# Small constants in one table, squares further ahead, warming matmuls, sums and gate product on POOL, last unit in quarters

## What is computed

```python
h = rmsnorm(x, g_mix)
u, q, k, v, og, zr, ga, gb = split(h @ w_in, (512, 256, 256, 512, 512, 16, 1024, 1024))
# branch A: four channel groups of u, trailing means over 2, 4, 8, 16 tokens minus the token,
pool = (((csum[t] - csum[t-w]) / w - u) @ w_group) * scale ; y_a = pool @ w_pool_proj
# branch B: gated linear attention, 4 heads, chunks of 64
loga = log_sigmoid(zr @ w_gk_up + b_gk) / 16 ; o = gla(q, k, v, loga, state)
y_b = (headnorm(o) * g_gla_norm * silu(og)) @ w_gla_proj
x = x + (sigmoid(ga) * y_a + sigmoid(gb) * y_b) @ w_out
x = x + (silu(gate) * up) @ w_ffn_out          # gate, up = rmsnorm(x, g_ffn) @ w_ffn_in
y = rmsnorm(x, g_final)                        # and the new pooling rows and GLA states
```

## Time and profile before

| | us |
|---|---|
| three runs: median (lowest, highest) | 910.1 (909.24, 910.98) |
| profiled execution, its own time | 910.94 |
| its span on the slowest core, 7 | 909.7 |
| spans of the other cores | 903.1 to 909.2 |
| PE busy / DVE / ACT / POOL on core 7 | 875.3 / 438.2 / 259.8 / 106.9 |

### The profile page before, as it was taken

How to read it: one execution, slowest core, us unless ns; L and a number is a source line. 1 busy time by engine, 2 the same in 40 slices (tenths; PEclk the granted TensorE clock), 3 DMA queues, 4 the chain that set the end, 5 groups by cost and what they waited for, 6 DMA issues and landing times.

```text
span 909.7 us, 14454 instructions; the slowest of 8 cores (903.1 to 909.7 us)
## 1 busy us (share of the span) xinstructions
PE 875.3 (96%) x4868; PEld 446.4 (49%) x4868; DVE 438.2 (48%) x735; ACT 259.8 (29%) x512; POOL 106.9 (12%) x214
## 2 busy tenths in 40 slices
PE   2898999999999999999999999999999999999996
PEld 1444556664565566556644444444444444444442
DVE  4578665656634422432256665565561332232146
ACT  4454343222332122112226524332231011101122
POOL 4300111102100000100022001120120000000002
PEclk9999999999999999999999999999999999999998
DMA  8964453828736916660875995343774753262504
GB/s 161 239 124 93 75 104 70 145 53 156 117 74 114 191 54 116 116 139 24 144 127 193 196 216 94 65 69 48 127 113 80 128 93 63 55 115 47 93 24 162
DMA packets 57627, 100.49 MB, mean 110 GB/s; under 512 B 41858, under 2 KB 42626, under 8 KB 50260
## 3 DMA queue, kind: packets, MB, share of 16 engines
q0 software_dynamic: 10272, 66.61, 41.3%
q1 hardware_dynamic: 47284, 32.96, 14.6%
HBM read 139.36 MB, written 11.53 MB: 166 GB/s over the span
## 4 chain that ended last, share of the span: by engine, by line
PE 92%; DMA 2%; DVE 2%; issue 2%; ACT 1%; POOL 1%; DVEq 0%; ACTq 0%; POOLq 0%
PE ps L419 88%; DMA ring<-w_a 2%; DVE R L316 1%; DVE R L320 1%; PE ps L763 1%; PE ps L744 0%; PE ps L541 0%; PE ps L721 0%; ACT R L310 0%; PE ps L764 0%; PE ps L532 0%; ACT R L312 0%; PE ps L1043 0%; ACT sgt L310 0%; PE ps L655 0%
## 5 line engine op out<-in xcount | busy, mean ns | idle before, releaser
L419 PE MATMUL ps<-hT,ring 128*128 128x368 bf16 (+2 forms) x2720 | 508.2, 344 | 5.8 <-ACT sgt L310 2.3
L419 PEld LDWEIGHTS ps<-hT,ring 128*128 128x128 bf16 x2720 | 261.2, 98 | 234.3 <-issue 12.6
L310 ACT ACTIVATE sgt<-ps 128x368 f32<-128x368 f32 (+2 forms) x207 | 109.6, 531 | 434.8 <-PE ps L419 374.1
L419 PE MATMUL ps<-ring,R 128*128 128x512 bf16 (+1 forms) x1020 | 222.5, 379 | 0.0
L316 DVE TENSOR_TENSOR R<-ps,sgt 128x368 bf16<-128x368 f32 (+1 forms) x110 | 66.1, 602 | 236.3 <-PE ps L419 228.9
L419 PEld LDWEIGHTS ps<-ring,R 128*128 128x128 bf16 (+1 forms) x1020 | 100.5, 99 | 118.9 <-issue 1.2
L316 DVE TENSOR_TENSOR xres<-xres,ps 128x512 f32<-128x512 f32 (+1 forms) x102 | 69.7, 686 | 67.2 <-PE ps L419 66.9
L419 PE MATMUL ps<-R,ring 128*128 128x368 bf16 (+1 forms) x320 | 70.6, 343 | 0.0
L312 ACT ACTIVATE R<-xres 128x1024 bf16<-128x1024 f32 (+2 forms) x44 | 45.6, 1036 | 86.3 <-DVE xres L320 43.4
L419 PE MATMUL ps<-ring,hT 128*128 128x512 bf16 (+1 forms) x272 | 62.5, 389 | 2.2 <-DMA ring<-w_a 2.2
L181 POOL DMA_DIRECT2D ring<-w_f x34 | 18.7, 549 | 293.4 <-PE ps L419 292.0
(11 more groups left out here) (104 smaller groups left out, 423.1 us busy)
## 6 DMA issues: line engine op xcount, KB each, us to landing
ring<-w_f POOLq DMA_DIRECT2D x30, 1024.0 KB, 11.9
ring<-w_a POOLq DMA_DIRECT2D x24, 1024.0 KB, 11.4
y_p<-xres SPq DMA_DIRECT2D x15, 512.0 KB, 2.9
xres<-xp POOLq DMA_DIRECT2D x8, 512.0 KB, 13.3
R<-xp SPq DMA_DIRECT2D x8, 512.0 KB, 6.3
xres<-xp SPq DMA_DIRECT2D x8, 512.0 KB, 28.9
ring<-w_f POOLq DMA_DIRECT2D x4, 768.0 KB, 11.9
R<-sgla SPq DMA_DIRECT2D x2, 1024.0 KB, 9.0
```

The source lines that it names most:

```text
L310: T.op('act', lambda e: e.activation(out=out, in_=in_, func=func, scale=scale, bias=bias), reads=rd, writes=wr)
L419: return [(lambda e, k=k: e.matmul(out, lhsT=lw(k), rhs=rx(k), start=(k == 0), stop=(k == K - 1))) for k in range(K)]
```

## The change

Constants: g_gla_norm, w_gk, b_gk and pool_scale are columns of one table `consts`, loaded with it from the POOL queue; the four loads of their own on SP are gone, and the negated b_gk is made by one DVE operation before the u projection. The first slab is issued after two x tiles, not three, with two more x tiles behind it. In pass one, squares and scales stand up to three and two units ahead of the transposes, and twelve matmuls on the zeroed tile qeZ (`warm`) stand before the first v projection. The product of `ogproj` in pass one and all of `swindows`, now right after the u projection of 'S', are POOL's. The last unit's second half is made in two quarters; its g_final product is taken before the scale is known, and the scaling is split over DVE and ACT, with a store from each of SP and ACT.

```diff
-    c = np.zeros((128, NCS), np.float32)
+    c = np.zeros((128, C_GN), np.float32)
...
-    gn_bc = sb("gn_bc", [128, 128])
+    gn_bc = cs[:, C_GN:C_GN + 128]
...
-    for u in range(3):
+    for u in range(2):
         load_x(0, u, 'pool')
     slab_topup()
+    for u in range(2, 4):
+        load_x(0, u, 'pool')
...
-    T.dma('sp', 'd_wgk', [(wgk_s[:, :], w_gk[:, :])], writes=[wgk_s[:, :]])
-    T.dma('sp', 'd_bgk', [(bgk[:, 0:2], b_gk[:, :])], writes=[bgk[:, 0:2]])
-    T.dma('sp', 'd_ps', [(pscale_c[:, :], pscale[:, :])], writes=[pscale_c[:, :]])
-    T.dma('sp', 'd_gn', [(gn_bc[:, :], g_gn.partition_broadcast(128))], writes=[gn_bc[:, :]])
...
-    loads = {0: [lambda: load_x(0, 3, 'pool')], 1: [lambda: load_x(0, 4, 'pool')],
-             2: [lambda: load_x(0, 5, 'pool'), lambda: load_x(0, 6, 'pool'), lambda: load_x(0, 7, 'pool'), load_cs, more_slab],
+    loads = {0: [lambda: load_x(0, 4, 'pool')], 1: [lambda: load_x(0, 5, 'pool')],
+             2: [lambda: load_x(0, 6, 'pool'), lambda: load_x(0, 7, 'pool'), load_cs, more_slab],
...
-            tt(G2[0:r, us, :].rearrange("p (h v) -> p h v", h=4), sg.rearrange("p (h v) -> p h v", h=4), g4, ALU.mult)
+            tt(G2[0:r, us, :].rearrange("p (h v) -> p h v", h=4), sg.rearrange("p (h v) -> p h v", h=4), g4, ALU.mult, eng='pool' if p == 0 else 'dve')
...
-                tt(ta[1 - bi][:, :, 0:ln], ta[bi][:, :, sh:sh + ln], ta[bi][:, :, 0:ln], ALU.add)
+                tt(ta[1 - bi][:, :, 0:ln], ta[bi][:, :, sh:sh + ln], ta[bi][:, :, 0:ln], ALU.add, eng='pool')
...
-            stt(pooled[:, g, SC:SC + NS].rearrange("p (s t) -> p s t", s=16), ta[bi][:, :, 0:4], 1.0 / w, E[:, :, 15:19],
-                ALU.mult, ALU.subtract)
-            if g == 3:
+            m4 = ta[1 - bi][:, :, 0:4]
+            T.op('pool', lambda e: e.tensor_scalar(out=m4, in0=ta[bi][:, :, 0:4], scalar1=1.0 / w, scalar2=None, op0=ALU.mult),
+                 reads=[ta[bi][:, :, 0:4]], writes=[m4])
+            tt(pooled[:, g, SC:SC + NS].rearrange("p (s t) -> p s t", s=16), m4, E[:, :, 15:19], ALU.subtract, eng='pool')
...
+            def warm(n):
+                b = nbank()
+                pe([(lambda e: e.matmul(banks[b][:, :], lhsT=qeZ[:, 0, 0:128], rhs=qeZ[:, 0, 0:512], start=True, stop=True))
+                    for _ in range(n)], [qeZ[:, 0, 0:512]], [banks[b][:, :]])
             n1s(0)
             n1s(1)
             n1a(0)
+            nb(0)
             n1s(2)
             n1a(1)
-            nb(0)
+            nb(1)
+            n1a(2)
+            nb(2)
+            warm(12)
             n1s(3)
-            n1a(2)
-            nb(1)
+            n1s(4)
             n1a(3)
-            nb(2)
-            nb(3)
             vp(0)
-            n1s(4)
-            vp(1)
             n1s(5)
             n1a(4)
+            vp(1)
+            nb(3)
+            n1s(6)
+            n1a(5)
             vp(2)
             for i in range(4, 9):
                 nb(i)
+                if i + 3 < 9:
+                    n1s(i + 3)
                 if i + 2 < 9:
-                    n1s(i + 2)
-                if i + 1 < 9:
-                    n1a(i + 1)
+                    n1a(i + 2)
                 vp(i - 1)
...
             for g in range(4):
                 uproj(ru, 'S', g)
+            for g in range(4):
+                swindows(g)
...
+            xg = f32v(R3, 0, 1024)
+
+            def final_q(u, k, c0_, n):
+                xt = xres[:, u, c0_:c0_ + n]
+                act(junk[:, c0_:c0_ + n], xt, AF.Square, scale=1.0 / 32.0, accum=gst[:, k:k + 1])
+                tt(xg[:, c0_:c0_ + n], xt, gfin_bc[:, c0_:c0_ + n], ALU.mult)
...
             def final_w(u):
+                T.op('pool', lambda e: e.tensor_scalar(out=gst[:, 5:6], in0=gst[:, 2:3], scalar1=gst[:, 4:5], scalar2=None, op0=ALU.add),
+                     reads=[gst[:, 2:3], gst[:, 4:5]], writes=[gst[:, 5:6]])
+                r_ = gst[:, 6:7]
+                tt(r_, gst[:, 5:6], negh[:, 0:1], ALU.pow, eng='pool')
                 t0 = p * PT + u * 128
-                for h in range(2):
-                    xt = xres[:, u, h * 512:(h + 1) * 512]
-                    stt(xt, xt, stat[:, u * 8 + 2:u * 8 + 3], gfin_bc[:, h * 512:(h + 1) * 512], ALU.mult, ALU.mult)
-                    T.dma('sp', f'd_z{h}', [(y_p[t0:t0 + 128, h * 512:(h + 1) * 512], xt)], reads=[xt])
+                ya, yb = xg[:, 0:640], xg[:, 640:1024]
+                T.op('dve', lambda e: e.tensor_scalar(out=ya, in0=ya, scalar1=r_, scalar2=None, op0=ALU.mult), reads=[ya, r_], writes=[ya])
+                act(yb, yb, AF.Copy, scale=r_)
+                T.dma('sp', 'd_z0', [(y_p[t0:t0 + 128, 0:640], ya)], reads=[ya])
+                T.dma('act', 'd_z1', [(y_p[t0:t0 + 128, 640:1024], yb)], reads=[yb])
...
                     if split:
-                        final_h(u, 0)
+                        final_q(u, 0, 0, 512)
+                        down(r1, 1, u, 0, 256)
+                        final_q(u, 1, 512, 256)
+                        final_l(u)
+                        down(r1, 1, u, 256, 256)
+                        final_q(u, 2, 768, 256)
+                        final(pend.pop(0))
+                        pend.append(u)
+                        continue
```

More of the change, by code:

```diff
@@ L33 @@
 C_RC = 946
-NCS = 1010
+C_GN = 1010
+C_GK = 1138
+C_BG = 1266
+C_PS = 1268
+C_NB = 1272
+NCS = 1274
 def _build_consts():
@@ L462, in build_program @@
     mset(Eb[:, :, 0:15], 0.0)
-    T.op('dve', lambda e: e.tensor_scalar(out=bgk[:, 2:4], in0=bgk[:, 0:2], scalar1=-1.0, scalar2=None, op0=ALU.mult),
-         reads=[bgk[:, 0:2]], writes=[bgk[:, 2:4]])
     def load_cs():
-        T.dma('pool', 'd_cs', [(cs[:, 128:NCS], cst[:, 128:NCS])], writes=[cs[:, 128:NCS]])
+        T.dma('pool', 'd_cs', [(cs[:, 128:C_NB], cst[:, 128:C_NB])], writes=[cs[:, 128:C_NB]])
     def load_hist():
@@ L545, in gk @@
                 for c, (out, sg) in enumerate(outs):
-                    act(sg, out, AF.Exp, scale=-1.0, bias=bgk[:, 2 + c:3 + c])
+                    act(sg, out, AF.Exp, scale=-1.0, bias=cs[:, C_NB + c:C_NB + c + 1])
                 for out, sg in outs:
@@ L635, in swindows @@
             E = xe[g]
[L636 removed]
+            tt(ta[0][:, :, 0:ln], E[:, :, lo + 1:lo + 1 + ln], E[:, :, lo:lo + ln], ALU.add, eng='pool')
             bi, sh = 0, 2
@@ L854, in build_program @@
             slab_topup()
+            T.op('dve', lambda e: e.tensor_scalar(out=cs[:, C_NB:C_NB + 2], in0=cs[:, C_BG:C_BG + 2], scalar1=-1.0, scalar2=None, op0=ALU.mult),
+                 reads=[cs[:, C_BG:C_BG + 2]], writes=[cs[:, C_NB:C_NB + 2]])
             for g in range(4):
                 uproj(ru, 'S', g)
+            for g in range(4):
+                swindows(g)
             for g in range(3):
@@ L945, in dense1 @@
             if has_s:
-                for i_, cost in enumerate(gate('a', 0, r0, rp, cols[:1])):
-                    if i_ < 4:
-                        swindows(i_)
-                    yield cost
+                yield from gate('a', 0, r0, rp, cols[:1])
                 for i_, cost in enumerate(gate('a', 0, r0, rp, cols[1:2])):
@@ L1154, in final_l @@
             def final_l(u):
-                col = stat[:, u * 8:u * 8 + 8]
-                T.op('pool', lambda e: e.tensor_scalar(out=col[:, 1:2], in0=col[:, 5:6], scalar1=col[:, 6:7], scalar2=EPS,
-                                                       op0=ALU.add, op1=ALU.add), reads=[col[:, 5:7]], writes=[col[:, 1:2]])
-                tt(col[:, 2:3], col[:, 1:2], negh[:, 0:1], ALU.pow, eng='pool')
+                T.op('pool', lambda e: e.tensor_scalar(out=gst[:, 4:5], in0=gst[:, 0:1], scalar1=gst[:, 1:2], scalar2=EPS,
+                                                       op0=ALU.add, op1=ALU.add), reads=[gst[:, 0:2]], writes=[gst[:, 4:5]])
```

35 lines of the change are left out of this document (12 added, 23 removed).

## The result

| | before | changed |
|---|---|---|
| median of 4 runs each, us | 910.54 (909.24 to 911.26) | 901.19 (900.85 to 901.72) |
| ratio, 95% interval | | 0.9899 (0.9882 to 0.9917) |
| profiled execution: its time, the slowest core's span | 910.94, 909.7 (core 7) | 901.29, 900.2 (core 0) |

The account below looks back on a forecast made before the run. The chain of waits was 92% PE work, so only four places where PE waits or runs slowly could pay: 3.4 + 2.5 + 1.2 + 0.8 = 7.9 off 910.94 gives 903.0 us, range 899 to 907.5.

Parts of the forecast that it names:

- Start, 3.4 forecast: Up to the first feature-major projection: earlier slab and squares ahead start it at 42.6 in place of 46.0.
- the four small SP loads ... are covered by the same wait ... nothing: At the start: removing these loads gains nothing, since PE's wait for the first slab and x tile covers them.
- the arrival near 22.6: At the start: the third x tile, now behind the first slab, arrives near 22.6 us.
- the warming matmuls themselves cost nothing: At the start: twelve matmuls fill PE's wait for an x tile; up to 2 us cost were it there at 21.
- Rival B: Start: clock not up when the slab lands, or x tiles later; gain 1.1 of 3.4, 905.3 us; chance 0.14.
- Gate product, 2.5 forecast: Output-gate projection, pass one: nine products on POOL cut a stall and clock price of 4.0 us to 1.5.
- If they take turns, a product starts every 1.6 us: Output-gate projection: POOL products of 1.25 us alternate with DVE's windows, 0.35 more each; ninth silu ends at 88.0.
- Rival A: Output-gate projection: DVE's windows run back to back and starve POOL; gain 0 to 0.5 there, 905.3 us; chance 0.18.
- Rival C: Output-gate projection: POOL products take over 3 us and delay the slab issue behind them; slower, 914.9 us; chance 0.05.
- Without the fall of the clock: Output-gate projection: 1.5 us of stall stays, but the 3.4 us at granted clock 0.51 behind it goes.
- swindows, 1.2 forecast: First gate block: 14 operations leave DVE's queue and PE's wait of 1.14 us goes; gain 0 to 2.
- End, 0.8 forecast: After the last matmul: quarters and split scaling gain 0.8 us (0.3 to 1.7), with POOL's operations held behind DVE.

Follow-up runs that it names:

- the last run: Four silu buffers on the changed kernel, plus separate 32-byte scalars for the last unit's square sums and the previous unit's last scaling in two DVE halves: 899.81 us, 0.9885.
- the best split: The changed kernel with pass one's gate product on POOL for the first five units and on DVE for the last four: 899.97 us, 0.9878.
- b_g2pool: The kernel before with one edit, pass one's gate products on POOL: 910.83 us, 1.0000.

## Why the prediction was right, and where not

- **The whole.** 903.0 forecast, 901.19 measured, in the range of 899 to 907.5. All four terms had the right sign. On core 7 the gate product and swindows were near their size, the start was half of what it gave, and the end gave nearly nothing. That the sum came near is in part luck: core 7 gained 11.9, and another core took 2.4 of it back.
- **Start, 3.4 forecast, 7.2 on core 7.** The step that failed is "the four small SP loads ... are covered by the same wait ... nothing", and with it the arrival near 22.6, which took the bytes per us of a slowed core as given. Putting the loads back costs 2.0 us of the kernel's time. On the five cores that were not slowed before, the start gained 3.5 to 4.7, near the forecast. The 0.8 for POOL's issues and the 3.8 from the tile's arrival to its transposes weren't what decided: with the tile at 18.07, TensorE is busy without a gap. That "the warming matmuls themselves cost nothing" holds for this order alone; where a late tile's transposes stand ahead of them they cost up to 4.8 us. Nor did they do what they were for: without them the u projection starts no later, and on core 7 only the last of the twelve took half of the first's time (0.22 us for 0.43), where I had named the last ones as a sign.
- **The order of squares.** I named it a cover ("squares two and three units ahead keep PE fed") and gave it no price. With what it does to the warming it is the largest part: with the slab first and the old order the kernel is slower than before, and with the old loads too it is 7.4 us slower than with the new order (909.14 against 901.78). How much of that is the order's alone isn't separated from the warming's place. Rival B (905.3) was wrong in its size, right that the x tiles' arrival is what counts.
- **Gate product, 2.5 forecast.** Measured 3.0 from the u projection to the recurrence with swindows on POOL, which cost 0.8 there; 1.3 to 1.4 of the 3.0 is the clock, for which the forecast had 1.7. Undone it costs 1.9 us. The size came for the wrong reason. "If they take turns, a product starts every 1.6 us" failed: DVE had its turn once, behind the first product, and then POOL kept the port for the eight others; its products start every 1.15 us, and no silu is late. The price went to DVE, and from it to the q projection (1.09 + 0.45) and to `sqb` (1.17 in place of 0.34): 2.4 us of wait in place of the 1.5 I kept. Rival A had the lock the other way round. The product's 1.25 was near (1.14 beside DVE's windows). The Trainium skill (GPSIMD Engine Reference, Performance versus the Vector engine) gave an estimate of 1.12 us for it; the trace agrees. Rival C is out: the slab behind the products is issued at 79.85, by 92 as forecast.
- **The rule of the port.** The Trainium skill (SBUF — State Buffer, Who interferes with whom) says that such operations of DVE and GpSimd contend, and, of another mode, that whoever issues first has the port for its instruction. The trace agrees on the lock in both directions: a 0.7 us DVE operation took 8.74. It shows besides that who comes next isn't fixed: DVE came in behind the first of POOL's nine products and between none of the others, and in the last run POOL came in between DVE's two halves on four cores (0.51 us) and not on the other four (1.10).
- **The clock.** "Without the fall of the clock" holds in the profile of the changed kernel, not in general: five kernels with the same three waits, and one with a first wait of 0.27, show it on 1 to 4 cores of 8, in the five at 1.3 to 1.5 us each. Before, it was behind the 2.34 on six cores.
- **swindows, 1.2 forecast**: 2.4 at the gate, less 0.8 at the q projection; the gate had two waits (1.14 and 0.99), and I had priced only the first; 1.6 to 1.7 net by the run without it. "POOL is idle where they go" left out whom they hold there, which I named only under the product.
- **End, 0.8 forecast, 0.1 to 0.3.** The held operations were seen; not seen was the wait of the last square for POOL's addition (0.71), which comes from the recorder: it tracks tiles in pieces of 32 bytes, so neighbouring columns of `gst` count as one. Taking that wait away gained nothing on four cores, where POOL's second addition ended after both of DVE's halves, and 0.3 on the four where it came in between them. The floor was the lock, except there.
- **The slowest core.** I summed core 7's losses and took them for the kernel's. With core 7's 11.9 us gone, another core's waits for DMA in pass two (2.2 us more) set the end.

## What to carry to other kernels

Work moved to GpSimd costs what it holds, not only what it takes: look for DVE operations with two SBUF inputs in the same stretch, and count the delay on the engine that waits for DVE. More buffers may do what the move does; here four in place of two, with the windows ahead, gave as much as the best split. Parts of a change that feed one queue in order (loads, squares, transposes) are to be priced together: the place of the slab made no clear difference with the new order of squares (901.19 and 901.78), and with the old one the new place lost nearly 5 us (913.89 and 909.14). When one core is last for a reason that the change removes, the gain ends at the next core.

## What was not expected of the hardware

- One DVE instruction of 0.7 us stood for 8.74 us, until GpSimd's queued products and the DMA issue behind them were done (10.18 us in b_g2pool). The operation ahead of it had been let in after one product. The other way round, a one-column addition of GpSimd behind two DVE halves took 1.10 us on four cores and 0.51 on four, in the same program.
- 0.13 MB in 576 small packets on the SP queue went with 1.15 MB less moved by the POOL queue in the first 24 us, but on two or three of the eight cores only, and not always the same.
- Behind three waits of 1.1, 0.45 and 1.2 us the granted clock fell on 1 to 4 of 8 cores in five kernels that have them (0.65 over 4 us); in others with the same waits (the changed kernel, and that with the small loads) on none, and on none in b_g2pool with 1.95, 0.45 and 1.17.
